# Three buffers instead of two for the split weight panels of a mixture-of-experts stage

## The chip, the cores and the metric

The kernel runs on one NeuronCore of a Trainium2 chip. The metric is the device time of one execution in microseconds (us). TensorE is called PE here, its weight loads PEld, VectorE DVE, ScalarE ACT, GpSimd POOL, and SyncE SP.

## The reference

Two blocks of a network on 256 tokens of width 2048, all in float32. The first is a convolution mixer and a SwiGLU feed-forward. The second is a mixer with gates, and then a hierarchical mixture of experts: a softmax picks one of 4 groups for each token, a second one two of the 4 experts of that group. Only this last part touches the change. Cut down:

```python
pg, g_idx = lax.top_k(p_group, 1)                      # one group of four
pe, e_idx = lax.top_k(softmax(sel_logits), 2)          # two of its four experts
hid = silu(einsum('td,edf->tef', t, w_gate)) * einsum('td,edf->tef', t, w_up)
y = einsum('tef,efd->td', hid * gate[:, :, None], w_down)   # e = 16 experts, f = 512
```

w_gate and w_up are 2048 x 512 for an expert, w_down is 512 x 2048: 12 MB for each of the 16 experts, all of which are read.

## The kernel before

**Precision.** A float32 product is made of three products of a reduced form (fp32r). ACT copies a weight panel into `whi` (the high half), DVE subtracts it from the panel and writes the remainder to `wlo` (the low half). The tokens are split the same way. PE then computes high tokens x high weights, low tokens x high weights, high tokens x low weights.

**Panels.** All weights pass in panels of 128 partitions x 2048 float32, 1 MB each. SP issues one transfer for each into a ring of raw buffers: four (`RING`, the tensor `raw`) in most of the kernel, six (`SLOTS`; `more_raw` holds the other two) in the expert jobs, where the memory of `xT` has come free. A raw buffer may be filled again when DVE has subtracted (`lo_ready`). `whi` and `wlo` have two buffers each, chosen by s % 2.

**Jobs.** The tokens of one group form a job. `GROUPS` is 4, and a group of more than 128 tokens would need one more job; in this trace there are four jobs, called 0 to 3 here. A job has 48 panels (`JOB`): for each of its 4 experts four gate panels, four up panels and four down panels, with the down panels of an expert behind the gate and up panels of the next. A gate or up panel takes 8 products with the high half (line L2635) and 4 with the low half (L2640); a down panel has both at L2652, and the last one of a job at L2666 and L2671. The first panel of the first job is `MOE` in the count of all panels.

**Who waits for whom.** Each engine works through its instructions in the order in which they are written, and counts on semaphores. For panel s of a job that begins at panel n:

- ACT (`expert_hi`, L724; for the first two panels of jobs 1 to 3, L1262) waits for PE's high products (`whi_used`) of the panel that had the buffer before, for DVE's subtraction of it (`lo_ready`), and for the transfer (`raw_in`).
- DVE (`expert_lo`, L1299) waits until PE is through with that earlier panel (`mm_done`) and ACT with this one (`hi_ready`).
- PE waits for `hi_ready`, runs the high products, adds to `whi_used`, waits for `lo_ready`, runs the low products, adds to `mm_done`.

```python
def expert_lo(n, s):
    v.wait_ge(mm_done, n + (s - 1))
    v.wait_ge(hi_ready, n + (s + 1))
    V.tensor_tensor(wlo[:, s % 2, :], expert_raw(s), whi[:, s % 2, :], ALU.subtract).then_inc(lo_ready, 1)
```

Between panels the engines do a job's other work, at fixed places of their order:

- After an expert's gate panels PE turns the hidden rows of the expert before (`turn_hidden`, L2678). ACT copies them (`turned_hi`, L1181) and then takes the sigmoid of the gate's sums (`silu_gate`, L1186), before it splits the seventh panel of the eight. DVE makes their low half (`turned_lo`, L1957) and multiplies (L2013).
- After the up panels DVE multiplies the hidden rows (`hidden`, L2019).
- Over the last eight panels of a job DVE scales four chunks of the next job's token rows (`scaled_row`, L1970). PE turns each chunk (L2627), ACT copies it (L1176), DVE makes its low half (`gathered_lo`, L1952).
- Over the first panels of a job DVE adds the down sums of the job before to its rows, in four chunks (L1995), ACT squares each (L1165), and the root follows (L728). DVE writes the scaled rows in the loop over the experts (L2008). POOL fetches the next job's rows and sends the finished ones.

Some of ACT's functions need another table, which takes an ACT_TABLE_LOAD.

In the first job the tokens' high halves, `tH`, lie in `xT` behind `more_raw`. PE gathers the job's tokens from them (L2615, `gath_done` counts the four parts); after that the memory is not used. The first two low halves of the first job are made by POOL.

Of the kernel before, what the change touches and what calls it, by code (L numbers as in the profile page):

```python
# [20 lines left out]
ALU = mybir.AluOpType  # L21
ACT = mybir.ActivationFunctionType
AX_X = mybir.AxisListType.X
F32 = mybir.dt.float32
F32R = mybir.dt.float32r
# [3 lines left out]
P = 128  # L29
PANEL = 2048  # L30
RING = 4
SLOTS = 6
BANK = 512
# [31 lines left out]
def build_program(  # L65
# [13 lines left out]
    NC = D // BANK  # L79
# [14 lines left out]
    DE = w_exp_gate_2.shape[3]  # L94
# [8 lines left out]
    B = A + 2 * KT  # L103
# [9 lines left out]
    MOE = G + KT  # L113
# [12 lines left out]
    with ctx:  # L126
        arena_at = -(-nc.sbuf_base // 32) * 32

        def sb(name, shape, dt=F32):
            return ctx.enter_context(nc.sbuf_tensor(name, shape, dt))  # L130

        def sem(name):
            return ctx.enter_context(nc.semaphore(name))

        BIG = FT * T
# [6 lines left out]
        whi = sb("whi", [P, 2, PANEL], F32R)  # L142
        wlo = sb("wlo", [P, 2, PANEL], F32R)
# [16 lines left out]
        ps = ctx.enter_context(nc.psum_tensor("ps", [P, 8, BANK], F32))  # L160
# [2 lines left out]
        xTA = xT[:, :].rearrange("p (k c) -> p k c", k=KT)  # L163
        xT5 = xT[:, 0:KT * BANK].rearrange("p (k c) -> p k c", k=KT)
        more_raw = nc.alloc_sbuf_tensor_at("more_raw", [P, SLOTS - RING, PANEL], F32, offset=arena_at + 4 * (BIG + (RING + 2 + 2) * PANEL))
        tH = xT[:, (SLOTS - RING) * PANEL:(SLOTS - RING) * PANEL + TOK * D].rearrange("p (t d) -> p t d", t=TOK)
        uext = big[:, 0:KT * EXT].rearrange("p (k c) -> p k c", k=KT)
        conv_at = KT * EXT + 32
# [17 lines left out]
        xg = moe_r[:, 0:2 * KT * P].rearrange("p (o k c) -> p o k c", o=2, k=KT)  # L186
# [56 lines left out]
        def expert_raw(s):  # L243

            return raw[:, s % SLOTS, :] if s % SLOTS < RING else more_raw[:, s % SLOTS - RING, :]

        def expert_landed(s, r):

            return r * 16 + (16 * (s // SLOTS + 1) + (16 * (MOE // RING) if s % SLOTS < RING else 0))

        raw_in = [sem(f"raw_in{i}") for i in range(SLOTS)]
        hi_ready = sem("hi_ready")
        lo_pool = sem("lo_pool")
        lo_ready = sem("lo_ready")
        mm_done = sem("mm_done")
        whi_used = sem("whi_used")
# [90 lines left out]
        gath_done = sem("gath_done")  # L347
# [359 lines left out]
        def _(a):  # L707
            own = Tally(act_own)
            fn = nc.scalar.activation
# [8 lines left out]

            def expert_hi(n, s, r):

                a.wait_ge(whi_used, n + (s - 1 - MOE))
                a.wait_ge(lo_ready, n + (s - 1 - B))
                a.wait_ge(raw_in[s % SLOTS], expert_landed(s, r))
                fn(whi[:, s % 2, :], expert_raw(s), ACT.Copy).then_inc(hi_ready, 1)  # L724

            def root(src, dst, scale, eps):

# [12 lines left out]
            for src, at in ((norm_mix_pre, V_PRE), (conv_b_in, V_BIN), (conv_b_dw, V_BDW), (conv_ln_g, V_LG),  # L740
                            (conv_ln_b, V_LB), (norm_ffn_pre, V_FPRE), (norm_mix_g_2, V_MIX2)):
                r = src.rearrange("a (k p) -> (a k) p", p=P)
# [336 lines left out]
            for q in range(4):  # L1079
                src = yc if q < 2 else tiles[:, UT:UT + CT, :]  # L1080
                k = (q % 2) * 4
# [80 lines left out]
            def z_square(count, c):  # L1162

                a.wait_ge(z_done, count + c + 1)
                fn(osq[c], orow[:, c * BANK:(c + 1) * BANK], ACT.Square,  # L1165
                   accum_out=st[:, SSQ + c:SSQ + c + 1]).then_inc(z_sq, 1)

            def z_root(count):
                a.wait_ge(z_sum, count)
                root(st[:, SS:SS + 1], st[:, RT:RT + 1], 1.0 / D, st[:, EPS_AT:EPS_AT + 1])  # L1170
# [12 lines left out]
            def silu_gate(done):  # L1183

                a.wait_ge(mm_done, done)
                fn(gsl, ps[:, 0, :], ACT.Sigmoid).then_inc(sig_g, 1)  # L1186
# [69 lines left out]
            def job(jb, more=True):  # L1256
                n = jb * JOB + MOE
                rj = jb * (JOB // SLOTS)
                for s in range(2):
                    a.wait_ge(mm_done, n + (s - 1))  # L1260
                    a.wait_ge(raw_in[s], expert_landed(s, rj))
                    fn(whi[:, s, :], expert_raw(s), ACT.Copy).then_inc(hi_ready, 1)  # L1262
                for c in range(NC):
                    expert_hi(n, 2 + c, rj)
                    z_square(jb * NC, c)
                silu_gate(n + 4)
                expert_hi(n, 6, rj)
                expert_hi(n, 7, rj)
                z_root(jb)
                job_rest(jb, n, more)  # L1270

            with a.Fori(1, last) as jb:
                job(jb)
            job(last, False)
            warm(5)
            for c in range(NC):
# [9 lines left out]
        def _(v):  # L1286
            own = Tally(dve_own)
            V = nc.vector
# [5 lines left out]

            def expert_lo(n, s):

                v.wait_ge(mm_done, n + (s - 1))
                v.wait_ge(hi_ready, n + (s + 1))
                V.tensor_tensor(wlo[:, s % 2, :], expert_raw(s), whi[:, s % 2, :], ALU.subtract).then_inc(lo_ready, 1)  # L1299

            def flat(x3):
                return x3.rearrange("p k c -> p (k c)")
# [430 lines left out]
            for q in range(4):  # L1733
                src = yc if q < 2 else tiles[:, UT:UT + CT, :]
                k = (q % 2) * 4
# [416 lines left out]
        def _(pe):  # L2152
            mm = nc.tensor.matmul
# [33 lines left out]
            for k in range(KT):  # L2187
# [7 lines left out]
                for t in range(TOK):  # L2195
                    i = mm(b[:, META + t * P:META + (t + 1) * P], h[:, t, k * P:(k + 1) * P], x_d[:, t, :], start=True, stop=True)
# [15 lines left out]
            for r in range(1, 6):  # L2212
                rows_in = P if r < 4 else (TAPS * KT - 3 * P if r == 4 else 3 * CT + KT)
                at = ps[:, 7, (r - 1) * P:(r - 1) * P + rows_in] if r < 5 else ps[:, 6, 0:rows_in]
                i = tr(at, vst[0:rows_in, r, :], ident[0:rows_in, 0:rows_in])
# [61 lines left out]
            def column_sum(half, src):  # L2277
                return mm(ps[:, 7, half * T:(half + 1) * T], ones[:, :], src, start=False, stop=True, skip_group_check=True)
# [22 lines left out]
            for m in range(2):  # L2301
                pe.wait_ge(sq_ready, PAIRS + m)
                i = column_sum(1, sq_buf[:, m * T:(m + 1) * T])
# [163 lines left out]
            for s in range(2):  # L2467
# [4 lines left out]
                for k in range(KT):  # L2472
                    i = mm(ps[:, 4 + s, 0:T], wlo[:, s, k * P:(k + 1) * P], xT5[:, k, 0:T], start=False, stop=(k == KT - 1))
# [13 lines left out]
            for q in range(8):  # L2487
# [8 lines left out]
                def banks(o, w):  # L2496
                    for t in range(TOK):
                        for c in range(2):
                            for k in range(2):
                                i = mm(ps[:, 2 * t + c, :], xT5[:, 2 * q + k, o * T + t * P:o * T + (t + 1) * P],  # L2500
                                       w[:, q % 2, k * SW + c * BANK:k * SW + (c + 1) * BANK],
                                       start=False, stop=True, skip_group_check=True)
                    return i
# [22 lines left out]
            for hd in range(HEADS):  # L2526
                for t in range(TOK):
                    at = (hd % 2) * T + t * P
                    i = mm(ps[:, hd // 2, at:at + P], vbuf[:, t, hd * P:(hd + 1) * P], wsT[:, hd, :], start=True, stop=True)
# [53 lines left out]
            for c in range(NC):  # L2583
                i = logits(1, c)
# [45 lines left out]
            def in_panel(n, s, q, bank):  # L2630

                pe.wait_ge(hi_ready, n + (s + 1))
                for o in range(2):
                    for k in range(4):
                        i = mm(ps[:, bank, :], xg[:, o, 4 * q + k, :], whi[:, s % 2, k * DE:(k + 1) * DE],  # L2635
                               start=(q == 0 and o == 0 and k == 0), stop=False)
                i.then_inc(whi_used, 1)
                pe.wait_ge(lo_ready, n + (s + 1 - B))
                for k in range(4):
                    i = mm(ps[:, bank, :], xg[:, 0, 4 * q + k, :], wlo[:, s % 2, k * DE:(k + 1) * DE],  # L2640
                           start=False, stop=(q == 3 and k == 3))
                i.then_inc(mm_done, 1)

# [4 lines left out]
            def down_panel(n, s, r, src):  # L2648

                def banks(o, w):  # L2650
                    for c in range(NC):
                        i = mm(ps[:, 4 + c, :], src[:, o, r, :], w[:, s % 2, c * BANK:(c + 1) * BANK],  # L2652
                               start=False, stop=True, skip_group_check=True)
                    return i
                pe.wait_ge(hi_ready, n + (s + 1))
                banks(0, whi)
                banks(1, whi).then_inc(whi_used, 1)
                pe.wait_ge(lo_ready, n + (s + 1 - B))
                banks(0, wlo).then_inc(mm_done, 1)

            def last_down_panel(n, s, r, src):

                pe.wait_ge(hi_ready, n + (s + 1))
                for o in range(2):
                    for c in range(NC):
                        i = mm(ps[:, 4 + c, :], src[:, o, r, :], whi[:, s % 2, c * BANK:(c + 1) * BANK],  # L2666
                               start=False, stop=True, skip_group_check=True)
                i.then_inc(whi_used, 1)
                pe.wait_ge(lo_ready, n + (s + 1 - B))
                for c in range(NC):  # L2670
                    i = mm(ps[:, 4 + c, :], src[:, 0, r, :], wlo[:, s % 2, c * BANK:(c + 1) * BANK],  # L2671
                           start=False, stop=True, skip_group_check=True)
                    i.then_inc(y_full if c < NC - 1 else mm_done, 1)

# [149 lines left out]
```

## Time and profile before

| | |
|---|---|
| median of 3 runs | 2301.48 us (2299.57 to 2301.8) |
| profiled execution, its own time | 2302.63 us |
| its span in the profile | 2300.9 us |
| busy: PE, PEld, DVE, ACT, POOL | 99%, 84%, 70%, 53%, 11% of the span |
| granted clock of PE, mean | 0.989 of full speed |
| DMA, mean over the span | 514.93 MB, 224 GB/s |
| expert jobs | about 1728 to 2289 us of the span |

The span reaches from the first to the last instruction. A share of busy time is a mean over stages with different limits, so the stage of the expert jobs is read by itself. A matmul's end is modelled; its weight load has both ends recorded.

### The profile page before, as it was taken

How to read it: one execution, taken by the hardware profiler on the slowest of the kernel's cores; microseconds unless marked ns; L12 is line 12 of the kernel's file. 1: busy time of each engine (PE TensorE's matmuls, PEld its weight loads, DVE VectorE, ACT ScalarE, POOL GpSimd, SP SyncE). 2: the span in 40 equal slices, each digit the busy share in tenths (PEclk: the TensorE clock that was granted, in tenths of full speed). 3: DMA queues.
4: the chain of work that ended last, by engine and by line, in shares of the span. 5: the costliest groups of instructions: out<-in, count | busy, mean ns of one | idle time of the engine just before them, and what ended most of it. 6: DMA issues, size and time to landing. Idle time of an engine off the chain costs nothing.

```text
span 2300.9 us, 34667 instructions
## 1 busy us (share of the span) xinstructions
PE 2267.9 (99%) x12099; PEld 1941.2 (84%) x12099; DVE 1610.5 (70%) x1910; ACT 1211.7 (53%) x1229; POOL 248.1 (11%) x107
## 2 busy tenths in 40 slices
PE   9999999999999999999999999999999999999997
PEld 8999688888888888888888888888887877878776
DVE  2999776656556654444586665567458898989987
ACT  4445356444444444344554444444346778687786
POOL 4898101000000000000100000000010000101001
PEclk9999799999999999999999999999989999999999
DMA  7665255666666665555567666655557999999995
GB/s 200 177 180 169 92 198 167 184 192 191 182 191 192 183 192 184 189 198 188 180 197 197 173 183 190 193 165 192 187 207 271 388 357 355 375 364 375 360 366 232
DMA packets 446150, 514.93 MB, mean 224 GB/s; under 512 B 12911, under 2 KB 407847, under 8 KB 410279
## 3 DMA queue, kind: packets, MB, share of 16 engines
q1 hardware_dynamic: 443268, 502.21, 67.1%
q0 software_dynamic: 2544, 11.66, 1.3%
q8 instruction: 39, 0.64, 0.1%
q10 hardware_dynamic: 272, 0.20, 0.0%
q14 instruction: 27, 0.22, 0.0%
HBM read 512.36 MB, written 6.29 MB: 225 GB/s over the span
## 4 chain that ended last, share of the span: by engine, by line
PE 88%; DVE 6%; issue 3%; ACT 3%; POOL 1%; DVEq 0%; ACTq 0%; POOLq 0%
PE ps L2426 25%; PE ps L2320 16%; PE ps L2431 13%; PE ps L2635 9%; PE ps L2652 5%; PE ps L2640 5%; DVE wlo L1299 2%; PE ps L2500 2%; PE ps L2239 2%; PE ps L2221 2%; PE ps L2222 2%; ACT whi L717 1%; DVE ps L1373 1%; PE ps L2333 1%; POOL wlo L547 1%
## 5 line engine op out<-in xcount | busy, mean ns | idle before, releaser
L717 ACT ACTIVATE whi<-raw 128x2048 fp32r<-128x2048 f32 x286 | 547.4, 1914 | 363.2 <-PE ps L2320 189.1
L1293 DVE TENSOR_TENSOR wlo<-raw,whi 128x2048 fp32r<-128x2048 f32 x248 | 567.7, 2289 | 205.3 <-ACT whi L717 205.3
L2426 PE MATMUL ps<-xT,whi 128*128 128x512 f32 x2656 | 638.3, 391 | 5.3 <-DVE xT L1737 4.3
L2426 PEld LDWEIGHTS ps<-xT,whi 128*128 128x128 f32 x2656 | 487.8, 189 | 99.7 <-issue 4.4
L2431 PEld LDWEIGHTS ps<-xT,wlo 128*128 128x128 f32 x2656 | 343.1, 191 | 14.3
L2431 PE MATMUL ps<-xT,wlo 128*128 128x256 f32 x2656 | 347.3, 283 | 0.0
L1299 DVE TENSOR_TENSOR wlo<-raw,whi 128x2048 fp32r<-128x2048 f32 x126 | 287.3, 2289 | 34.8 <-ACT whi L724 30.3
L978 ACT ACTIVATE wk<-ps 128x256 f32<-128x256 f32 x184 | 68.8, 383 | 449.2 <-PE ps L2431 448.9
L724 ACT ACTIVATE whi<-raw 128x2048 fp32r<-128x2048 f32 x120 | 228.5, 1916 | 66.0 <-PE ps L2652 32.9
L2320 PE MATMUL ps<-whi,act 128*128 128x512 f32 x1088 | 260.7, 392 | 0.0
L2635 PE MATMUL ps<-whi,moe_r 128*128 128x512 f32 x1024 | 258.0, 394 | 0.3 <-issue 0.3
L2320 PEld LDWEIGHTS ps<-whi,act 128*128 128x128 f32 x1088 | 206.2, 190 | 44.0 <-issue 0.8
L2635 PEld LDWEIGHTS ps<-whi,moe_r 128*128 128x128 f32 x1024 | 191.2, 189 | 42.1 <-issue 2.5
L1563 DVE TENSOR_TENSOR wk<-ps,wk 128x256 f32<-128x256 f32 x184 | 78.0, 424 | 125.7 <-ACT wk L978 123.7
L1373 DVE SCALAR_TENSOR_TENSOR ps<-big,vT,ps 128x256 f32<-128x256 f32 x410 | 162.1, 481 | 0.0
L1299 DVE TENSOR_TENSOR wlo<-more_raw,whi 128x2048 fp32r<-128x2048 f32 x64 | 146.3, 2291 | 14.6 <-ACT whi L724 14.4
L547 POOL TENSOR_TENSOR wlo<-raw,whi 128x2048 fp32r<-128x2048 f32 x32 | 148.2, 4633 | 30.7 <-ACT whi L717 30.4
L724 ACT ACTIVATE whi<-more_raw 128x2048 fp32r<-128x2048 f32 x64 | 122.8, 1918 | 47.2 <-PE ps L2635 34.4
L2640 PE MATMUL ps<-wlo,moe_r 128*128 128x512 f32 x512 | 139.8, 395 | 3.0 <-DVE wlo L1299 2.4
L1440 DVE TENSOR_TENSOR act<-big,act 128x256 fp32r<-128x256 f32 x60 | 25.3, 425 | 161.4 <-ACT act L896 161.4
L2320 PE MATMUL ps<-wlo,act 128*128 128x512 f32 x544 | 134.4, 389 | 0.0
L2221 PE MATMUL ps<-xT,whi 128*128 128x272 f32 x480 | 121.6, 289 | 0.9 <-DVE vT L1334 0.9
(329 smaller groups left out, 2259.2 us busy)
## 6 DMA issues: line engine op xcount, KB each, us to landing
raw<-in_w_in SPq DMA_DIRECT2D x72, 1024.0 KB, 5.4
raw<-in_w_exp_up SPq DMA_DIRECT2D x56, 1024.0 KB, 6.9
raw<-in_ffn_w_gate SPq DMA_DIRECT2D x44, 1024.0 KB, 5.5
raw<-in_ffn_w_up SPq DMA_DIRECT2D x44, 1024.0 KB, 5.5
raw<-in_ffn_w_down SPq DMA_DIRECT2D x44, 1024.0 KB, 4.8
raw<-in_w_exp_gate SPq DMA_DIRECT2D x40, 1024.0 KB, 6.8
raw<-in_conv_w_in SPq DMA_DIRECT2D x32, 1024.0 KB, 6.0
more_raw<-in_w_exp_down SPq DMA_DIRECT2D x32, 1024.0 KB, 7.5
```

Of the source, the lines that this page charges most:

```text
L547: pool.tensor_tensor(wlo[:, s % 2, :], raw[:, s, :], whi[:, s % 2, :], ALU.subtract).then_inc(lo_pool, 1)
L717: fn(whi[:, s % 2, :], raw[:, s % RING, :], ACT.Copy).then_inc(hi_ready, 1)
L724: fn(whi[:, s % 2, :], expert_raw(s), ACT.Copy).then_inc(hi_ready, 1)
L1293: V.tensor_tensor(wlo[:, s % 2, :], raw[:, s % RING, :], whi[:, s % 2, :], ALU.subtract).then_inc(lo_ready, 1)
L1299: V.tensor_tensor(wlo[:, s % 2, :], expert_raw(s), whi[:, s % 2, :], ALU.subtract).then_inc(lo_ready, 1)
L1373: ins = V.scalar_tensor_tensor(out=accs[m], in0=src, scalar=w, in1=accs[m], op0=ALU.mult, op1=ALU.add)
L2221: mm(ps[:, bank, 0:TM], w, xTA[:, k, 0:TM], start=(k == 0), stop=False)
L2320: i = mm(ps[:, t * NC + c, :], act[:, s % 2, part, t * P:(t + 1) * P], w[:, s % 2, c * BANK:(c + 1) * BANK], start=False, stop=True, skip_ ...
L2426: mm(ps[:, bank, :], whi[:, s % 2, at:at + P], xT5[:, k0 + k, :], start=(k == 0), stop=False)
L2431: i = mm(ps[:, bank, 0:T], wlo[:, s % 2, at:at + P], xT5[:, k0 + k, 0:T], start=False, stop=(k == count - 1))
L2635: i = mm(ps[:, bank, :], xg[:, o, 4 * q + k, :], whi[:, s % 2, k * DE:(k + 1) * DE], start=(q == 0 and o == 0 and k == 0), stop=False)
L2640: i = mm(ps[:, bank, :], xg[:, 0, 4 * q + k, :], wlo[:, s % 2, k * DE:(k + 1) * DE], start=False, stop=(q == 3 and k == 3))
```

## The change

`whi` and `wlo` get a third buffer in the expert jobs. It is a new tensor `third` with two panels, in `xT` right behind `more_raw`, which is where the first job's `tH` lies. Two helpers choose the buffer by s % 3, and 48 is a multiple of 3, so that the choice is the same in each job. The waits on the panel that had the buffer before move from s-2 to s-3, which is one less in each count. Panel 2 of the first job is the first in `third`; its split waits for the end of the gather instead.

```diff
+        third = nc.alloc_sbuf_tensor_at("third", [P, 2, PANEL], F32R, offset=arena_at + 4 * (BIG + (SLOTS + 2 + 2) * PANEL))
...
+        def expert_whi(s):
+
+            return whi[:, s % 3, :] if s % 3 < 2 else third[:, 0, :]
+
+        def expert_wlo(s):
+
+            return wlo[:, s % 3, :] if s % 3 < 2 else third[:, 1, :]
...
             def expert_hi(n, s, r):
 
-                a.wait_ge(whi_used, n + (s - 1 - MOE))
-                a.wait_ge(lo_ready, n + (s - 1 - B))
+                if isinstance(n, int) and n == MOE and s == 2:
+                    a.wait_ge(gath_done, NC)
+                else:
+                    a.wait_ge(whi_used, n + (s - 2 - MOE))
+                    a.wait_ge(lo_ready, n + (s - 2 - B))
                 a.wait_ge(raw_in[s % SLOTS], expert_landed(s, r))
-                fn(whi[:, s % 2, :], expert_raw(s), ACT.Copy).then_inc(hi_ready, 1)
+                fn(expert_whi(s), expert_raw(s), ACT.Copy).then_inc(hi_ready, 1)
...
                 for s in range(2):
-                    a.wait_ge(mm_done, n + (s - 1))
+                    a.wait_ge(mm_done, n + (s - 2))
                     a.wait_ge(raw_in[s], expert_landed(s, rj))
...
             def expert_lo(n, s):
 
-                v.wait_ge(mm_done, n + (s - 1))
+                v.wait_ge(mm_done, n + (s - 2))
                 v.wait_ge(hi_ready, n + (s + 1))
-                V.tensor_tensor(wlo[:, s % 2, :], expert_raw(s), whi[:, s % 2, :], ALU.subtract).then_inc(lo_ready, 1)
+                V.tensor_tensor(expert_wlo(s), expert_raw(s), expert_whi(s), ALU.subtract).then_inc(lo_ready, 1)
```

In `in_panel`, `down_panel` and `last_down_panel` PE reads `expert_whi(s)` and `expert_wlo(s)` in place of the buffers by s % 2; its waits and its order are as before. SP's and POOL's code isn't touched.

## Rows read from the trace of the kernel before

**Rows 1.** The windows view, job 1: busy us of each engine, granted clock, DMA share, GB/s

```profile
1894.80:2035.00 140.20, 139.37 (x621) 111.27 (x621) 127.77 (x85) 108.28 (x78) 6.83 (x2) 1.00 0.97 365
```

**Rows 2.** The waits view of PEld, 1757 to 2289 us: total us, times, longest

```profile
PEld ps L2640 <- DVE wlo L1299: 8.4, 22, 0.7
PEld ps L2652 <- DVE wlo L1299: 7.4, 18, 0.8
```

**Rows 3.** The timeline, an undisturbed panel: start us, us, engine, line

```profile
1792.84 1.92 ACT L724 ACTIVATE whi<-more_raw 128x2048 fp32r<-128x2048 f32 x1 [0.82 <-PE ps L2635]
...
1794.80 2.29 DVE L1299 TENSOR_TENSOR wlo<-more_raw,whi 128x2048 fp32r<-128x2048 f32 x1 [0.45 <-ACT whi L724]
1794.98 0.87 PEld L2640 LDWEIGHTS ps<-wlo,moe_r 128*128 128x128 f32 x4
...
1795.89 1.77 PEld L2635 LDWEIGHTS ps<-whi,moe_r 128*128 128x128 f32 x8
...
1797.70 0.87 PEld L2640 LDWEIGHTS ps<-wlo,moe_r 128*128 128x128 f32 x4
```

**Rows 4.** The timeline, behind a turn of the hidden rows

```profile
1906.61 1.92 ACT L724 ACTIVATE whi<-raw 128x2048 fp32r<-128x2048 f32 x1 [0.78 <-PE ps L2635]
...
1907.19 0.60 PE L2678 MATMUL ps<-ident,tmp 128*128 128x128 f32 x4
...
1908.44 0.58 ACT L1181 ACTIVATE moe_r<-ps 128x512 fp32r<-128x512 f32 x1
...
1909.04 1.28 ACT L1186 ACT_TABLE_LOAD   x1
...
1910.82 3.71 ACT L724 ACTIVATE whi<-raw 128x2048 fp32r<-128x2048 f32 x2
...
1912.77 4.49 DVE L1299 TENSOR_TENSOR wlo<-raw,whi 128x2048 fp32r<-128x2048 f32 x2 [0.71 <-ACT whi L724]
1912.90 1.77 PEld L2635 LDWEIGHTS ps<-whi,moe_r 128*128 128x128 f32 x8
...
1915.11 0.76 PEld L2640 LDWEIGHTS ps<-wlo,moe_r 128*128 128x128 f32 x4 [0.44 <-DVE wlo L1299]
...
1915.92 1.80 PEld L2635 LDWEIGHTS ps<-whi,moe_r 128*128 128x128 f32 x8
```

**Rows 5.** The lines view of DVE, job 1: xcount, busy us, mean ns, idle before

```profile
L1970 DVE SCALAR_TENSOR_TENSOR tmp<-h,st,gB 128x512 f32<-128x512 f32 x4 | 4.5, 1136 | 0.0
...
L1952 DVE TENSOR_TENSOR moe_r<-ps,moe_r 128x512 fp32r<-128x512 f32 x4 | 2.7, 683 | 0.0
```

**Rows 6.** The timeline, the start of job 2 and the longest wait

```profile
2012.02 1.77 PEld L2635 LDWEIGHTS ps<-whi,moe_r 128*128 128x128 f32 x8
...
2016.60 0.68 DVE L1995 TENSOR_TENSOR moe_o<-ps,h 128x512 f32<-128x512 f32 x1
...
2019.40 0.68 DVE L1995 TENSOR_TENSOR moe_o<-ps,h 128x512 f32<-128x512 f32 x1
...
2132.90 0.76 PEld L2652 LDWEIGHTS ps<-wlo,moe_r 128*128 128x128 f32 x4 [0.83 <-DVE wlo L1299]
```

**Rows 7.** The timeline, the first job's panels 2 and 4

```profile
1735.99 2.28 DVE L1299 TENSOR_TENSOR wlo<-raw,whi 128x2048 fp32r<-128x2048 f32 x1
...
1738.33 0.76 PEld L2640 LDWEIGHTS ps<-wlo,moe_r 128*128 128x128 f32 x4 [2.19 <-DVE wlo L1299]
...
1746.02 0.76 PEld L2640 LDWEIGHTS ps<-wlo,moe_r 128*128 128x128 f32 x4 [0.77 <-DVE wlo L1299]
```

**Rows 8.** The windows view, timeline and landing: the transfers

```profile
1970.00:1985.00 15.00, 15.00 (x70) 12.40 (x69) 13.48 (x8) 11.46 (x8) 0.00 (x0) 1.00 1.02 418
...
2108.79 0.33 SPq L494 DMA_DIRECT2D raw<-in_w_exp_up  x1
...
DMA to landing us min/median/max: 12.0/12.0/12.0
...
2121.32 1.92 ACT L724 ACTIVATE whi<-raw 128x2048 fp32r<-128x2048 f32 x1 [0.80 <-PE ps L2635]
```

More of the change, by code:

```diff
@@ L2634, in in_panel @@
                     for k in range(4):
-                        i = mm(ps[:, bank, :], xg[:, o, 4 * q + k, :], whi[:, s % 2, k * DE:(k + 1) * DE],
+                        i = mm(ps[:, bank, :], xg[:, o, 4 * q + k, :], expert_whi(s)[:, k * DE:(k + 1) * DE],
                                start=(q == 0 and o == 0 and k == 0), stop=False)
@@ L2639, in in_panel @@
                 for k in range(4):
-                    i = mm(ps[:, bank, :], xg[:, 0, 4 * q + k, :], wlo[:, s % 2, k * DE:(k + 1) * DE],
+                    i = mm(ps[:, bank, :], xg[:, 0, 4 * q + k, :], expert_wlo(s)[:, k * DE:(k + 1) * DE],
                            start=False, stop=(q == 3 and k == 3))
@@ L2651, in banks @@
                     for c in range(NC):
-                        i = mm(ps[:, 4 + c, :], src[:, o, r, :], w[:, s % 2, c * BANK:(c + 1) * BANK],
+                        i = mm(ps[:, 4 + c, :], src[:, o, r, :], w[:, c * BANK:(c + 1) * BANK],
                                start=False, stop=True, skip_group_check=True)
@@ L2655, in down_panel @@
                 pe.wait_ge(hi_ready, n + (s + 1))
-                banks(0, whi)
-                banks(1, whi).then_inc(whi_used, 1)
+                banks(0, expert_whi(s))
+                banks(1, expert_whi(s)).then_inc(whi_used, 1)
                 pe.wait_ge(lo_ready, n + (s + 1 - B))
-                banks(0, wlo).then_inc(mm_done, 1)
+                banks(0, expert_wlo(s)).then_inc(mm_done, 1)
             def last_down_panel(n, s, r, src):
@@ L2665, in last_down_panel @@
                     for c in range(NC):
-                        i = mm(ps[:, 4 + c, :], src[:, o, r, :], whi[:, s % 2, c * BANK:(c + 1) * BANK],
+                        i = mm(ps[:, 4 + c, :], src[:, o, r, :], expert_whi(s)[:, c * BANK:(c + 1) * BANK],
                                start=False, stop=True, skip_group_check=True)
@@ L2670, in last_down_panel @@
                 for c in range(NC):
-                    i = mm(ps[:, 4 + c, :], src[:, 0, r, :], wlo[:, s % 2, c * BANK:(c + 1) * BANK],
+                    i = mm(ps[:, 4 + c, :], src[:, 0, r, :], expert_wlo(s)[:, c * BANK:(c + 1) * BANK],
                            start=False, stop=True, skip_group_check=True)
```

## The prediction

> **What bounds the kernel now.** I first read the page's forty slices. From about 1750 us on they are another kernel: the rows of DMA and GB/s jump, DVE's and ACT's rise, PE's stays full. That stretch is the expert jobs, the only code that the diff touches. The trace holds four jobs of 48 panels, 192 in all. The windows view then says which engine sets the pace: in job 1 (the second) PE is busy 139.37 of 140.20 us at a granted clock of 1.00, DVE 127.77, ACT 108.28, and the core moves 365 GB/s [rows 1]. PE is the bound; a "busy" PE can still lose time, because the end of a matmul is modelled. So the timeline of PE's weight loads (PEld) is the one to read: each matmul has one load, and a gap between loads is lost time.
>
> Where nothing is late, the eight products with the high half take 1.81 us, the four with the low half 0.91 us, and a panel 2.72 us [rows 3]. The waits view of PEld over 1757 to 2289 us holds 22 waits of 8.4 us in the gate/up panels and 18 of 7.4 us in the down panels for DVE's subtraction that makes the low half [rows 2]. No wait for a high half and none for a DMA is in it. So 40 waits, 15.8 us, stand between PE and its full pace.
>
> They cost less than they last. In row group 4 the high products start at 1912.90, so the low ones were due at 1914.71; they start at 1915.11 (0.40 late), and the next panel would start at 1915.92 where 1915.62 was due: the four loads after a wait go 0.10 faster. A wait noted as 0.44 costs 0.30 us; the note is 0.14 too long. Forty waits cost 15.8 - 40 x 0.14 = 10.2 us. This is what is at stake here.
>
> **Why the low half is late.** For panel 22 of job 0, ACT starts the high half at 1792.84, 0.82 us after idling for PE, ends it at 1794.76; DVE takes 1794.80 to 1797.09; PE wants the low half at 1797.70 [rows 3]. The margin is 0.61 us. With two buffers ACT may not start panel s until PE's high products of s-2 have been read, so neither ACT nor DVE can build up more than this 0.61 us, though a panel needs only 1.92 us of ACT and 2.29 of DVE out of 2.72. Any other DVE work above 0.61 us plus the slack is passed on to PE: 1.14 us for a gain-scaled chunk of token rows, 0.68 for the low half of gathered columns [rows 5].
>
> **The change part by part.** Nothing is computed anew, no instruction is added but the choice of a buffer, which is made when the program is built. The panel arithmetic, the DMA count (192 of 1 MB) and their order stay. So no cost is added in work; all of it is a shift of waits.
>
> 1. *Waits of ACT and DVE one panel back* (whi_used, lo_ready and mm_done at s-2 in place of s-1). ACT and DVE may run up to 2.72 us further ahead. The margin goes from 0.61 to at most 3.33 us. The longest of the forty waits in the timeline is 0.83 us, in panel 41 of job 2 [rows 6]; the burst behind it has used up 0.61 + 0.83 = 1.4 us of margin: under 3.33. Over a job DVE has 140.2 - 127.8 = 12.4 us idle [rows 1]; after a gain of 3.4 a job there are still 9 left, so the lead can be rebuilt: (2.72 - 2.29) = 0.43 us a panel.
>
> 2. *The in-order stretches*, where more buffers don't help by themselves, since ACT's and DVE's queues hold an instruction that needs PE. I walk the three kinds.
>  After PE turns the hidden rows (once an expert), ACT's order is: split of the panel before, copy of the turned rows, a table load, the sigmoid, split of the next panel. In row group 4 the split at 1906.61 runs to 1908.53 and pushes the copy to 1908.44, though the turn's last matmul ended at 1907.79; the load follows at 1909.04, and the splits at 1910.82, DVE at 1912.77, ending 1915.06 for a due time of 1914.71. With a third buffer the split of 1906.61 is done a panel earlier, the copy starts at about 1907.9, and the rest moves with it by 0.5 us: the low half ends at about 1914.5. The 0.35 us that it was too late is covered, by 0.15 us only.
>  At the end of a job DVE carries four chunks of scaled rows (4 x 1.14), four low halves of gathered columns (4 x 0.68), a hidden-row product (0.7) and the low half of the turned rows (0.7) beside eight panels: 8 x 2.29 + 8.7 = 27.0 us, against 8 x 2.72 + about 2.5 of PE's turns = 24.3. It runs 2.7 us behind over this stretch; the lead of up to 3.33 takes it up with little left. The same order of instructions laid out by hand, with each one's wait on PE or ACT, gives every low half in time, the tightest (panel 45) by about 0.0 us.
>  At the start of a job DVE takes a chunk of the finished rows (0.68) between panels, and chunk to chunk is 2.80 us (2016.60 to 2019.40) [rows 6] for PE's 2.72: DVE loses 0.08 a panel for four panels. The first chunk stands 4.6 us behind PE's first load of the job (2012.02) now [rows 6], and by the same laying out about 3 us behind it after. Panel 9, which comes after the root of the final norm and two table loads on ACT, is again in time by about 0.0 us.
>  I therefore take 0.3 us a job for what the two tight places still cost: 3 x 0.3 = 0.9 us. Its bounds are 0 (the walk is right) and 4.2 us (rival 1).
>
> 3. *Panel 2 of the first job waits for the gather's end* instead of for whi_used and lo_ready. Its split is not held up by either: the low half of panel 2 starts at 1735.99, behind DVE's low half of the last gathered columns, and PE waits 2.19 us for it until 1738.33 [rows 7]. That order is not edited. This wait, and one of 0.77 us two panels on [rows 7], which lies behind a chain of small routing instructions in DVE's order, stay. Gain at the start: 0; bounds 0 and the 2.7 us that both cost. PE's own order has the whole gather ahead of panel 0, which is two panels earlier, so the new wait costs nothing.
>
> 4. *The transfers.* A panel's raw buffer is freed by DVE, so the transfers start earlier by as much as DVE runs ahead, and are wanted earlier by as much. The total supply must rise from 48 panels in 140.2 us (2.92 us each) to 48 in 136.8 (2.85). A stretch with the queue full moved 418 GB/s over 15 us: 1.0486 MB in 2.51 us [rows 8]. So there is room. The tightest place is after the fetch of the next job's rows: a panel issued at 2108.79 landed 12.0 us later, at 2120.79, and ACT took it at 2121.32 [rows 8], 0.53 us later. ACT will meet the transfer there and wait, but it spends its lead, not PE's time. Cost 0; bound above by rival 3.
>  The Trainium skill (DMA: Bandwidth & Descriptors, Where 436 GB/s comes from) says that for transfers from HBM to SBUF the HBM side binds at about 358 GB/s. By that rule the jobs, at 365 GB/s, would already be at their limit and the sum of this change 0. The row of 418 GB/s over 15 us disagrees; the section above it on the same page gives 358 as the share with both cores of a pair streaming.
>
> **The sum.** 10.2 - 0.9 + 0 = 9.3 us. The profiled execution took 2302.63 us (span 2300.9 and 1.7 around it), so 2293.3 for such a one; its time is 1.15 over the median of the three runs, 2301.48, so the median comes to 2292.2 us, 0.40% less.
>
> **The rivals.**
> 1. *ACT's serial stretches keep their stalls.* Four places a job (two turns of hidden rows with a table load, the loop's start with another, the root of the final norm) are set by ACT's order, not by buffers. For it: before the split at 1910.82 ACT did not idle [rows 4]. Against: the copy ahead of it was delayed by a split that the third buffer moves. At 0.30 each, with 3.5 jobs' worth: 4.2 us stay, the gain is 6.0, the time 2295.5.
> 2. *The change does nothing that counts*: DMA share is 0.97 in job 1 [rows 1], supply is at its limit, and the waits for DVE turn into waits for transfers. Time 2301. The Trainium skill's 358 GB/s (same section) would make this the case. Against: 418 GB/s [rows 8], and even at the tightest place a landed panel lies 0.53 us before ACT takes it, while ACT's idle time is named by PE.
> 3. *Slower*: with ACT, DVE and transfers bunched at the job's ends, the transfers come less evenly than now, and PE waits for high halves. The place is panels 38 to 41 of jobs 1 and 2 after the fetch, with 0.53 us in hand. It decides when the mean landing interval exceeds today's 2.92 us a panel; at 2.95 it costs 0.03 x 188 = 5.6 us: 2307. Against: 2.51 us a panel was reached in just such a stretch, behind the fetch of job 1.
> 4. *More*: the start's two waits vanish too, and no tight place costs: 10.2 + 2.7 = 12.9, 2288.6. Against: DVE's order there is not touched.
>
> **How the numbers follow.** Forecast 0.66, rival 1 0.17, rival 2 0.10, rival 3 0.05, rival 4 0.02. The likeliest gives 2292.2. Its own range is 2290.5 to 2294.5. The range for eight in ten reaches from rival 4's 2288.5 to 2299, halfway from rival 1 to no change. A measurement of this kernel tells about 0.2% (4.6 us) from no change, so "faster" is below 2296.9: the forecast, rival 4 and, with 6.0 us of gain, most of rival 1: 0.81. "Same" gets rival 2 and the weak end of rival 1: 0.14. Slower: 0.05.
>
> **What the changed profile would show.** The waits view of PEld over the jobs should fall from 15.8 us in 40 waits to under 3 us, with those left behind panels 9 and 45 or after a hidden turn. A job should last about 137 us. The start should still show its waits of some 2.2 and 0.8 us. ACT's idle time should be named more by transfers or by older panels. Splits should begin up to 2.7 us further ahead of PE; ACT's 1.92 and DVE's 2.29 us should not change. I would be wrong if PE shows waits for high halves or ACT waits of microseconds for landings that reach PE, if the splits become longer, or if the waits after hidden turns stay at 0.4.

## The result and the profile after

The change makes the kernel faster: 2287.16 us, the median of 5 runs (2285.26 to 2288.57), against 2301.65 (2299.57 to 2301.96). The comparison of the runs gives a ratio of 0.9942, with a 95% interval of 0.9931 to 0.9953 (the two medians alone give 0.9937). The forecast was 2292.2 with a range of 2288.5 to 2299: right in sign and mechanism, too small by 5 us, and the median lies below the range. The profiled execution took 2285.31 us.

The page of the changed kernel: the span, and busy time, share and instructions of the engines.

```profile
span 2283.6 us, 34678 instructions
...
PE 2254.0 (99%) x12099; PEld 1943.3 (85%) x12099; DVE 1607.3 (70%) x1910; ACT 1208.3 (53%) x1229; POOL 248.0 (11%) x107
```

The work of DVE and ACT is what it was (1610.5 and 1211.7 us before), so nothing was saved in work. PE's line has 13.9 us less in it (2267.9 before) for the same 12099 matmuls: it counts time in which a matmul runs slowly or waits, so the sum of busy time alone doesn't say where it went.

The windows view of jobs 0, 1 and 2 (cut at the first product of each job's bank clearing): length, busy us of PE, PEld, DVE, ACT and POOL, granted clock, DMA share, GB/s.

```profile
1750.80:1886.90 136.10, 135.90 (x617) 112.00 (x617) 124.77 (x86) 102.13 (x74) 2.24 (x1) 1.00 0.96 373
1886.90:2023.50 136.60, 136.60 (x622) 112.38 (x622) 126.73 (x86) 107.18 (x78) 6.83 (x2) 1.00 0.97 374
2023.50:2160.10 136.60, 136.60 (x622) 112.41 (x622) 127.20 (x86) 107.76 (x78) 6.83 (x2) 1.00 0.97 378
```

Job 1 lasts 136.6 us against 140.2 [rows 1], and PE is busy in all of it. PEld's busy time rose from 111.27 to 112.38 for the same loads, and that is no loss: the four loads behind a wait take 0.76 us together in place of 0.87 [rows 3, rows 4], and there are fewer of them. DMA moves 374 GB/s against 365.

The waits view of PEld over the jobs of the changed kernel: total us, times, longest.

```profile
PEld ps L2647 <- issue: 1.5, 3, 0.6
PEld ps L2238 <- issue: 1.1, 3, 0.4
PEld ps L2647 <- ACT whi L736: 0.8, 2, 0.4
```

The forty waits for DVE of [rows 2] are gone, every one. What is left stands where it stood before: the clearing of the banks, the loops' ends. The two waits put down to ACT's split are no late high halves. Each is the 0.42 us behind the clearing of the banks, which is in the kernel before as well and is called "issue" there.

The timeline behind a turn of the hidden rows, the place of [rows 4] in the same job.

```profile
1898.66 0.58 PEld L2690 LDWEIGHTS ps<-ident,tmp 128*128 128x128 f32 x4
1898.89 0.60 PE L2690 MATMUL ps<-ident,tmp 128*128 128x128 f32 x4
...
1899.52 0.60 ACT L1193 ACTIVATE moe_r<-ps 128x512 fp32r<-128x512 f32 x1 [2.01 <-PE ps L2690]
1900.14 1.28 ACT L1198 ACT_TABLE_LOAD   x1
...
1901.43 0.60 ACT L1198 ACTIVATE tmp<-ps 128x512 f32<-128x512 f32 x1
...
1901.92 1.91 ACT L736 ACTIVATE third<-raw 128x2048 fp32r<-128x2048 f32 x1
...
1903.87 2.29 DVE L1311 TENSOR_TENSOR third<-raw,third 128x2048 fp32r<-128x2048 f32 x1 [1.12 <-ACT third L736]
...
1904.59 1.77 PEld L2647 LDWEIGHTS ps<-third,moe_r 128*128 128x128 f32 x8
...
1906.08 2.28 DVE L1311 TENSOR_TENSOR wlo<-raw,whi 128x2048 fp32r<-128x2048 f32 x1
...
1906.40 0.87 PEld L2652 LDWEIGHTS ps<-third,moe_r 128*128 128x128 f32 x4
...
1908.28 2.29 DVE L1311 TENSOR_TENSOR wlo<-more_raw,whi 128x2048 fp32r<-128x2048 f32 x1
```

ACT now idles ahead of the copy (L1193) and starts it at 1899.52, where PE's turn ends at 1899.49. In [rows 4] it began 0.65 us after the end of the turn, held up by a split. The rest of ACT's order is as before. DVE's low half of panel 14 runs from 1903.87 to 1906.16, and PE wants it at 1906.40: 0.24 us to spare, where it was 0.35 late. The subtractions behind it start 2.20 us apart (1906.08, 1908.28), though each is listed with 2.28 or 2.29 us. So DVE gains 0.52 us on a panel of 2.72 us when it doesn't wait.

The transfers at their tightest place, after the fetch of the next job's rows in job 2. In [rows 8] ACT's idle time was still named by PE; now ACT's timeline has:

```profile
2107.98 1.92 ACT L736 ACTIVATE whi<-more_raw 128x2048 fp32r<-128x2048 f32 x1 [0.44 <-DMA more_raw<-in_w_exp_down]
2110.52 1.92 ACT L736 ACTIVATE third<-more_raw 128x2048 fp32r<-128x2048 f32 x1 [0.62 <-DMA more_raw<-in_w_exp_down]
2113.01 1.92 ACT L736 ACTIVATE whi<-raw 128x2048 fp32r<-128x2048 f32 x1 [0.57 <-DMA raw<-in_w_exp_down]
```

In panels 40 to 42 ACT waits for transfers, 0.4 to 0.6 us each, and PE sees nothing of it.

The start of the first job, where the forecast said nothing would change (DVE's low half of panel 2, then PEld):

```profile
1729.83 2.28 DVE L1311 TENSOR_TENSOR third<-raw,third 128x2048 fp32r<-128x2048 f32 x1
...
1732.16 0.77 PEld L2652 LDWEIGHTS ps<-third,moe_r 128*128 128x128 f32 x4 [2.19 <-DVE third L1311]
...
1735.22 0.77 PEld L2652 LDWEIGHTS ps<-wlo,moe_r 128*128 128x128 f32 x4 [0.47 <-DVE wlo L1311]
...
1739.84 0.76 PEld L2652 LDWEIGHTS ps<-wlo,moe_r 128*128 128x128 f32 x4 [2.02 <-DVE wlo L1311]
```

The 2.19 us are the same as in [rows 7]. The 0.77 became 0.47 and 2.02: in this execution the granted clock was 1.00 where the one before had a short stretch at a lower level (a mean of 0.66 over 1738 to 1743 us), and PE met DVE's routing chain sooner. The change has no part in it: the unchanged kernel shows 0.46 and 1.99 us in one of its later executions, at a clock of 1.00. From the first product of panel 0 to the clearing of the banks both kernels take 27.8 us, so the start gave nothing.

**Where the time went.** The two profiled spans differ by 17.3 us, more than the medians. At the first product of panel 0 the changed kernel is already 6.2 us ahead (1722.0 against 1728.2), and it is 5.0 of that ahead at the first product of the convolution's output projection (257.1 against 262.1), in code that the change doesn't touch. From panel 0 to the last panel it takes 549.6 us against 560.7: 11.1 us. So two questions are open: what are the 6 us, and which part of the change gave the 11.

### The profile page after: what moved, and what is told of

The parts are those of the page before. It is cut to its first block, busy times and chain, and to the rows that moved or that the text cites. A ratio compares the mean times of both kernels' runs of the same rounds, so it can differ in the third digit from the quotient of the medians.

```text
span 2283.6 us, 34678 instructions
## 1 busy us (share of the span) xinstructions
PE 2254.0 (99%) x12099; PEld 1943.3 (85%) x12099; DVE 1607.3 (70%) x1910; ACT 1208.3 (53%) x1229; POOL 248.0 (11%) x107
## 4 chain that ended last, share of the span: by engine, by line
PE 92%; DVE 3%; issue 2%; ACT 2%; POOL 1%; DVEq 0%; ACTq 0%; POOLq 0%
PE ps L2438 25%; PE ps L2332 16%; PE ps L2443 13%; PE ps L2647 10%; PE ps L2664 7%; PE ps L2652 5%; PE ps L2512 2%; PE ps L2251 2%; PE ps L2233 2%; PE ps L2234 2%; ACT whi L726 1%; DVE ps L1385 1%; PE ps L2345 1%; POOL wlo L556 1%; PE ps L2174 1%
## 5 line engine op out<-in xcount | busy, mean ns | idle before, releaser
L726 ACT ACTIVATE whi<-raw 128x2048 fp32r<-128x2048 f32 x286 | 547.4, 1914 | 359.6 <-PE ps L2332 184.8
L1305 DVE TENSOR_TENSOR wlo<-raw,whi 128x2048 fp32r<-128x2048 f32 x248 | 567.8, 2289 | 205.4 <-ACT whi L726 205.4
L1311 DVE TENSOR_TENSOR wlo<-raw,whi 128x2048 fp32r<-128x2048 f32 x94 | 214.2, 2288 | 3.9 <-ACT whi L736 3.5
L736 ACT ACTIVATE whi<-raw 128x2048 fp32r<-128x2048 f32 x88 | 168.1, 1914 | 32.2 <-PE ps L2647 23.1
L2647 PE MATMUL ps<-whi,moe_r 128*128 128x512 f32 x672 | 168.2, 392 | 0.2 <-issue 0.2
L556 POOL TENSOR_TENSOR wlo<-raw,whi 128x2048 fp32r<-128x2048 f32 x32 | 147.8, 4623 | 31.2 <-ACT whi L726 30.9
L2647 PEld LDWEIGHTS ps<-whi,moe_r 128*128 128x128 f32 x672 | 124.8, 188 | 26.0 <-issue 0.6
L2233 PE MATMUL ps<-xT,whi 128*128 128x272 f32 x480 | 121.8, 289 | 0.9 <-DVE vT L1346 0.9
L2234 PE MATMUL ps<-xT,whi 128*128 128x272 f32 x480 | 121.5, 287 | 0.0
L2332 PEld LDWEIGHTS ps<-wlo,act 128*128 128x128 f32 x544 | 102.1, 188 | 21.2
L649 POOL TENSOR_TENSOR wlo<-raw,whi 128x2048 fp32r<-128x2048 f32 x4 | 18.3, 4589 | 833.7 <-DVE h L1498 833.4
```

Source lines behind the costliest of these rows:

```text
L556: pool.tensor_tensor(wlo[:, s % 2, :], raw[:, s, :], whi[:, s % 2, :], ALU.subtract).then_inc(lo_pool, 1)
L726: fn(whi[:, s % 2, :], raw[:, s % RING, :], ACT.Copy).then_inc(hi_ready, 1)
L736: fn(expert_whi(s), expert_raw(s), ACT.Copy).then_inc(hi_ready, 1)
L1305: V.tensor_tensor(wlo[:, s % 2, :], raw[:, s % RING, :], whi[:, s % 2, :], ALU.subtract).then_inc(lo_ready, 1)
L1311: V.tensor_tensor(expert_wlo(s), expert_raw(s), expert_whi(s), ALU.subtract).then_inc(lo_ready, 1)
L2233: mm(ps[:, bank, 0:TM], w, xTA[:, k, 0:TM], start=(k == 0), stop=False)
```

## The experiments

The stage "jobs" below is the time from the first product of panel 0 to the start of the last product of the last panel, read from each run's own profile. "Ahead" is the start of panel 0.

**Controls.** No edit; the two kernels again, first in several runs and later in one profiled execution more.

> The kernel before, unchanged, as a control. The profile of the changed kernel stands 17.3 us ahead of the one before when the last panel is through: 6.2 us of it at 335 us of the span, long ahead of the expert jobs, and 11.1 within them. Theory A: the 6.2 us are chance: the stretch in which PE is granted half the clock around 245 to 280 us was 23.9 us long in one execution and 10.2 in the other, and its length differs between executions of one kernel; in some executions of this control it is short too, and the first panel of the expert jobs starts near 1722 instead of 1728. Theory B: the stretch is long in every execution of this kernel and short in those of the changed one, since the program's size or place changed; then this control shows 1728 again and a ratio of 1.000. The time by both: 2300 to 2302, by A with some runs down to 2296.

> The changed kernel again, unchanged. Expert jobs, from the first load of panel 0 to the end of the last panel: 549.7 us as in its first profile, within 0.5. The part ahead of them: by theory A between 1722 and 1728 us, by theory B 1722. Time 2285 to 2289 by B, up to 2291 by A.

Measured: the kernel before 2302.23 us (2298.96 to 2304.03, 12 runs), ahead 1728.2, jobs 560.9; the same kernel, run beside it as the reference of the comparison, 2301.35 with 23 runs from 2296.3 to 2304.15; ratio 1.0002 (0.9993 to 1.0010). The changed kernel 2290.56 us (2285.48 to 2293.1, 6 runs), ratio 0.9946 (0.9932 to 0.9959), ahead 1726.9, jobs 549.9. The jobs repeat to 0.2 us. The part ahead differed by 4.9 us between two executions of the changed kernel.

> The kernel before, one look more at the length of the half-clock stretch: 10 to 24 us by theory A, with jobs of 560.8 us in either case; always 20 or more by theory B.

> The changed kernel, one look more: jobs of 549.8 us; the stretch of half clock ahead 10 to 24 us long.

Measured: the kernel before ahead 1723.7, jobs 560.8; the changed one ahead 1727.7, jobs 549.7. So this time the unchanged kernel had the short part ahead and the changed one the long. The windows view at the end of the convolution (the last three columns are granted clock, DMA share, GB/s) for the kernel before:

```profile
245.00:255.00 10.00, 10.00 (x20) 4.62 (x19) 4.42 (x7) 1.37 (x3) 0.00 (x0) 0.66 0.29 105
255.00:265.00 10.00, 10.00 (x30) 6.04 (x29) 8.26 (x15) 2.86 (x7) 0.56 (x1) 0.66 0.39 128
265.00:275.00 10.00, 10.00 (x46) 8.28 (x45) 6.94 (x13) 5.19 (x6) 0.00 (x0) 1.00 0.29 100
```

and for the changed kernel, on the same chip:

```profile
245.00:255.00 10.00, 10.00 (x16) 4.67 (x15) 3.65 (x7) 1.22 (x2) 0.00 (x0) 0.50 0.28 105
255.00:265.00 10.00, 10.00 (x21) 4.60 (x20) 8.26 (x15) 2.75 (x7) 0.56 (x1) 0.50 0.43 135
265.00:275.00 10.00, 10.00 (x40) 8.03 (x40) 3.61 (x10) 2.73 (x4) 0.00 (x0) 0.87 0.18 76
```

The first runs 20 us at a mean of 0.66 and is then at full speed; the second is at 0.50, the lower of TensorE's two levels, 1.2 GHz, for the whole 20 us and beyond (0.87 over the next ten). The unchanged kernel had 0.50 there too in its two executions before this one. What PE does there is the same in both, column sums and products with one row. Theory A holds: the length of this stretch varies from execution to execution, in both kernels.

**The high half alone, the low half alone.**

```diff
 # hi_only, on the changed kernel
-            return wlo[:, s % 3, :] if s % 3 < 2 else third[:, 1, :]
+            return wlo[:, s % 2, :]
...
-                v.wait_ge(mm_done, n + (s - 2))
+                v.wait_ge(mm_done, n + (s - 1))
```

> Three high halves, two low halves as before: ACT may run a panel further ahead, DVE waits as before for PE to be through with panel s-2. By my forecast's reasoning the low half is late from DVE's bursts (end and start of a job) and from ACT's order (after the turn of the hidden rows, after the root). With ACT alone ahead, the second kind goes and the first stays. Of the 11.0 us that the jobs gained, I expect 3 to 6. Rival: both halves of the change are needed together, since DVE's own wait on PE keeps it from using an early high half: then under 2 us. Second rival: the high half alone gives nearly all, over 9.

Measured: 2288.28 us (2285.85 to 2293.41), ratio 0.9944 (0.9931 to 0.9957), ahead 1723.7, jobs 550.2. PEld's only waits for DVE in the jobs behind the start, and DVE's waits for PE:

```profile
PEld ps L2664 <- DVE wlo L1311: 0.5, 2, 0.3
```

```profile
DVE wlo L1311 <- PE ps L2652: 18.2, 46, 0.4
...
DVE wlo L1311 <- PE ps L2664: 3.8, 10, 0.4
```

My figure of 3 to 6 us was wrong; the second rival holds, the high half alone gives 10.7 of the 11.1. DVE does wait for PE now, 56 times and 22 us in all, and it costs 0.4. I had the margins of the two buffers confused. With two high halves ACT may start a split when PE has used the one two panels back, and ACT's 1.92 and DVE's 2.29 us both lie behind that. With two low halves only DVE's 2.29 us lie behind the wait: the timeline of this kernel has it at one panel as

```profile
1785.98 2.29 DVE L1311 TENSOR_TENSOR wlo<-raw,whi 128x2048 fp32r<-128x2048 f32 x1 [0.43 <-PE ps L2664]
1787.29 0.87 PEld L2652 LDWEIGHTS ps<-wlo,moe_r 128*128 128x128 f32 x4
```

and PE wants this low half at 1790.01, behind the next panel's. That is 1790.01 - 1788.27 = 1.7 us of margin, where the longest wait of before had asked for 1.4.

```diff
 # lo_only, on the changed kernel: two high halves with the waits of before
-            return whi[:, s % 3, :] if s % 3 < 2 else third[:, 0, :]
+            return whi[:, s % 2, :]
...
-                    a.wait_ge(whi_used, n + (s - 2 - MOE))
-                    a.wait_ge(lo_ready, n + (s - 2 - B))
+                a.wait_ge(whi_used, n + (s - 1 - MOE))
+                a.wait_ge(lo_ready, n + (s - 1 - B))
...
-                    a.wait_ge(mm_done, n + (s - 2))
+                    a.wait_ge(mm_done, n + (s - 1))
```

> Three low halves, two high halves as before: DVE may run ahead, but ACT still waits for PE's high products of s-2 and gives DVE a high half only 2.9 us before PE wants the low one. I expect at most 1 us of the 11.0, since the waits view says that DVE idled for ACT's split and not for PE. Rival: DVE's bursts gain from it as well, 3 to 6 us.

Measured: 2297.84 us (2296.15 to 2303.74, 12 runs), ratio 0.9993 (0.9982 to 1.0004), ahead 1724.9, jobs 560.8. The waits of PEld over the jobs behind the start, and DVE's:

```profile
PEld ps L2661 <- DVE wlo L1308: 5.2, 15, 0.7
PEld ps L2649 <- DVE third L1308: 5.0, 13, 0.5
PEld ps L2649 <- DVE wlo L1308: 3.2, 8, 0.7
...
PEld ps L2661 <- DVE third L1308: 2.3, 3, 0.8
```

```profile
DVE third L1308 <- ACT whi L733: 25.0, 33, 2.2
DVE wlo L1308 <- ACT whi L733: 19.9, 48, 0.9
```

39 waits of 15.7 us, as in [rows 2]; DVE waits for ACT's split as before. The third low half gives nothing by itself.

**How much lead there is.** DVE makes one low half twice, that of the first down panel (16 and 28) of two experts in each job, 8 times in all.

```diff
+                if twice is not None:
+                    V.tensor_tensor(wlo[:, s % 2, :], expert_raw(s), whi[:, s % 2, :], ALU.subtract).then_inc(lo_once, 1)
+                    v.wait_ge(lo_once, twice)
```

> The kernel before, with one subtraction of DVE (2.29 us, and about 0.1 for a wait on itself) done twice, in the first down panel of each expert in the loop: 8 places in the four jobs, one panel ahead of the hidden rows' product and, in jobs 1 to 3, of two scaled chunks. With two high halves DVE's margin is 0.61 us, and in jobs 1 to 3 it is used up there. Expected: the jobs grow by 13 to 19 us over 560.7. It measures the margin, not a computed result: the output is the same.

> Three high and two low halves, with the same double subtraction. High halves give 0.61 + 2.72 = 3.3 us of margin; the wait of DVE for PE to be through with panel s-2 leaves 0.91 or less: lo(s) may start when panel s-2 is through, and PE wants it 2.72 + 1.81 = 4.5 us later, so 2.2 us of margin beside the subtraction. If that is the bound, a burst of 2.4 us alone costs 0.2, and 2.4 + 2.2 us in jobs 1 to 3 about 1.5 at each of 6 places: jobs 550.1 + 5 to 11. If two low halves were no bound at all: + 0 to 3.

> Three high and three low halves, with the same double subtraction. Margin 3.3 us from the high halves and 4.9 from the low ones. If the third low half is worth something when DVE's bursts are longer, the jobs grow less than with two: 549.8 + 0 to 6, and below the run with three high halves alone. Rival: the same as that one, then the third low half is worth nothing here either.

Measured, in one execution each: 2313.88, 2298.72 and 2301.64 us; jobs 572.8, 560.0 and 558.6 us, so + 12.0, + 9.8 and + 8.8 over the same kernels without the edit. The line with most of PEld's waits in each, in that order:

```profile
PEld ps L2656 <- DVE wlo L1303: 20.7, 26, 1.8
```

```profile
PEld ps L2668 <- DVE wlo L1315: 13.0, 23, 1.2
```

```profile
PEld ps L2668 <- DVE wlo L1315: 10.9, 18, 1.2
```

The first is below what I expected, the second inside, the third above. With three buffers of each a burst of 2.4 us should have vanished in a margin of 3.3. In job 0 it did: its two places have no wait, and the job got 0.1 us longer. The 18 waits stand at the six places of jobs 1 to 3, and each of these jobs got 2.9 us longer, 1.5 us a place. So the 3.3 us are not there in panel 16 of those jobs. The timeline of the third kernel shows it, in job 1:

```profile
1917.53 1.77 PEld L2668 LDWEIGHTS ps<-whi,moe_r 128*128 128x128 f32 x8
...
1918.11 2.29 DVE L1315 TENSOR_TENSOR wlo<-more_raw,whi 128x2048 fp32r<-128x2048 f32 x1
1920.32 2.29 DVE L1315 TENSOR_TENSOR third<-more_raw,third 128x2048 fp32r<-128x2048 f32 x1
...
1920.45 0.76 PEld L2668 LDWEIGHTS ps<-wlo,moe_r 128*128 128x128 f32 x4 [1.15 <-DVE wlo L1315]
```

PE's high products begin at 1917.53, so the low ones were due at 1919.34. The low half of panel 16 is there only at 1920.4. Without the second subtraction it would have been there at 1918.1, so the lead was 1.2 us, not 3.3. Two panels before, behind the turn of the hidden rows, the lead is 0.24 us (above), and it is 0.2 with two low halves as well: ACT has to wait there for PE's turn and then has a copy, a table load and a sigmoid ahead of its next split. From there it grows by the 0.52 us that DVE gains on a panel. In job 0 the same turn has no table load behind it (ACT copies at 1762.44, takes the sigmoid at 1762.93 and splits at 1763.41). The changed kernel without the double subtraction shows there, again for panel 14:

```profile
1765.36 2.29 DVE L1311 TENSOR_TENSOR third<-raw,third 128x2048 fp32r<-128x2048 f32 x1 [0.18 <-ACT third L736]
...
1769.30 0.87 PEld L2652 LDWEIGHTS ps<-third,moe_r 128*128 128x128 f32 x4
```

The low half is there at 1767.65, a lead of 1.65 us, and by panels 19 to 23 it has grown to 3.3 or 3.4 us, where the buffers end it. The third low half is worth 1.4 us of jobs in this case, 1.0 of them in job 0, where the lead can pass 1.7 us before the burst. It is worth 0.4 without the double subtraction.

**A better start.** DVE's order at the first job's start, on the kernel with three high halves alone.

```diff
-            gathered_lo(0, 3, FIRST_TURN[3])
             expert_lo(MOE, 2)
-            chosen_logits()
+            gathered_lo(0, 3, FIRST_TURN[3])
             expert_lo(MOE, 3)
-            chosen_experts()
+            chosen_logits()
             expert_lo(MOE, 4)
+            chosen_experts()
```

> Three high and two low halves, and DVE's order at the first job's start: the low half of panel 2 ahead of the low half of the last gathered columns, the low halves of panels 3 and 4 each ahead of the routing chain that preceded it. The 2.19 us that PE waits in panel 2 should go (the high half is there 2 us earlier, and DVE idles), and of the 0.47 and 2.02 us behind it some 1 to 1.5 us. Jobs 547 to 548.5 against 550.1. Rival: DVE is the bound over the whole stretch up to panel 8, and the gain at panel 2 is lost again before the gates: 549.5 to 550.

Measured: 2287.57 us (2285.15 to 2292.47), ratio 0.9948 (0.9933 to 0.9962), jobs 549.1. PEld's waits at the start:

```profile
1732.89 0.76 PEld L2652 LDWEIGHTS ps<-wlo,moe_r 128*128 128x128 f32 x4 [0.28 <-DVE wlo L1311]
...
1736.08 0.76 PEld L2652 LDWEIGHTS ps<-wlo,moe_r 128*128 128x128 f32 x4 [0.56 <-DVE wlo L1311]
...
1739.15 0.76 PEld L2652 LDWEIGHTS ps<-wlo,moe_r 128*128 128x128 f32 x4 [0.45 <-DVE wlo L1311]
...
1743.77 0.76 PEld L2652 LDWEIGHTS ps<-wlo,moe_r 128*128 128x128 f32 x4 [2.02 <-DVE wlo L1311]
1745.44 0.52 PEld L2697 LDWEIGHTS ps<-wk,moe_r 128*128 128x128 f32 x4 [0.91 <-DVE wk L1959]
```

The 2.19 us of panel 2 shrank to 0.28, and the same time came back behind it: the rival holds for the most part. The jobs missed the 547 to 548.5 us that I expected. DVE's routing chain has to end before the gates, wherever it stands. The gain is 1.0 us by the stages, and too small for the times to tell: this kernel, the one with three high halves and the changed one are alike.

**The stretch of half clock, filled.** Three matmuls on all rows of the array ahead of each bias product but those of bank 7, on both kernels. The trace has 42 of them, so 14 sets and not the 12 of the expectation.

```diff
+                if bank != 7:
+                    for _ in range(3):
+                        mm(ps[:, bank, 0:P], ones[:, :], ones[:, :], start=True, stop=True)
```

> The kernel before with three more matmuls of 128x128 on all rows of the array ahead of each of 12 one-row bias products between the convolution and its output projection, where PE is granted half the clock for 10 to 24 us. Their results are overwritten. By theory A (the length of that stretch differs between executions, whatever the kernel) full-array work there removes or fixes the stretch: the spread of times, 8 us so far (2296.0 to 2304.2), shrinks to some 2 us, and the first panel of the expert jobs starts at the same time in this kernel and in the changed one with the same edit. The edit itself costs up to 9 us of PE and gives back up to 10. If the stretch stays, nothing is learned from the level.

> The changed kernel with the same edit. Theory A: the part ahead of the expert jobs as in the kernel above, within 1 us, and the time 11.0 us below it (10.5 to 11.5), which is the change by itself. Theory B (the change also shortens the part ahead by some 3 to 6 us): 14 us or more below it.

Measured: 2303.48 us (2300.24 to 2312.07, 12 runs) and 2294.98 (2289.03 to 2302.47, 12 runs), both slower than without the edit. The spread did not shrink, it grew to 12 and 13 us, so the pair did not isolate the change by its times (8.5 us between the medians, 11.2 between the lowest). Theory A had expected the same part ahead in both, within 1 us; it was 1725.8 and 1734.1. Over 245 to 265 us the mean clock was 0.83 in the first and 0.69 in the second, so the stretch was altered and not removed. The jobs took 560.8 and 549.7 us, 11.1 apart, as without the edit.

## Why the prediction was wrong

**What holds.** The bound (PE), the place (the low half is late behind ACT's split), the sign, DMA and the tightest place of the transfers, where ACT waits and PE doesn't, the unchanged 2.19 us at the start, the 0.2 us that a turn of the hidden rows with a table load leaves to spare, and a job of about 137 us were as forecast. By the stages the change is worth 11.1 us.

**The sum was 9.3.** The stage gave 11.1. The 0.9 us for the two tight places, panels 9 and 45, measured 0: no wait stands there. Panel 45's low half is ready within 0.1 us of when it is wanted in jobs 0 to 2, as laid out; panel 9's is 0.6 to 1.1 us early in jobs 1 to 3, where I had 0.0. The forty panels that had a noted wait became 10.5 us shorter, against the forecast 10.2: each wait cost 0.13 us less than its note, short ones and long ones alike, against the 0.14 taken from one of them. Another 0.6 us came from the other panels, which the sum had at nothing: 0.14 in the last panel of job 0, the rest under 0.05 us a panel, too short for the waits view to list. Together 1.8 us; 2290.4 would have been inside the range.

**The step that failed** is in "The sum": the forecast was set on 2301.48, the median of three runs, as if the rest of the kernel stood still. It doesn't. The part ahead of the jobs ended between 1722.0 and 1729.4 us in the profiled executions without the fill, and 6.6 of these 7.4 us arose between the first bias product (near 241 us) and 341 us, around the stretch at half clock. The unchanged kernel took 2296.0 to 2304.15 us over all its 75 runs, the changed one 2285.3 to 2293.1 over its 12: both ends are 11 us apart, as the jobs are. The first three runs of before fell between 2299.6 and 2301.8, the first five of after in their lower half. My range had no term for this, and it was worth 3.4 us: the medians differ by 14.5, the stage by 11.1. That it is chance and not the change's work is shown by the pair of executions in which the unchanged kernel had the shorter part ahead (1723.7 against 1727.7). The later runs agree: the medians of the second comparison are 10.8 us apart.

**Part 1** credited both halves of the change with the lead. It is the third high half; the third low half alone gives 0, and 0.4 us on top of the other.

**The margin of 3.3 us** is what the buffers allow, and panels 19 to 23 of job 0 reach it. It is no figure for the whole job: behind a turn of the hidden rows with a table load, two in each of jobs 1 to 3, it is 0.24. The forecast for those places was right because it was worked out there, and the double subtraction showed what the general figure is worth elsewhere. The rate at which the lead comes back was put too low, at 0.43 us a panel from the listed 2.29 us; subtractions in a row start 2.20 us apart, which gives 0.52.

**The rivals.** The first (ACT's serial stretches keep 4.2 us) fell: those waits are gone, if by 0.24 us. The second and third (supply of transfers) fell: 378 GB/s in job 2. The Trainium skill's 358 GB/s (DMA: Bandwidth & Descriptors, Where 436 GB/s comes from) would have left no gain; the trace disagrees, with 378 GB/s averaged over a whole job. The fourth was right that no tight place would cost; the start's two waits, which it had vanish, stayed.

## What to carry to other kernels

Where one value passes two engines on its way to a third, the buffer to add is the one whose release lies at the head of the chain: its wait covers both engines' work, and the second buffer's covers only the last. A deeper buffer gives lead only up to the next instruction in the same queue that needs the consumer, so the lead has to be worked out at those places, with what follows in that queue (here 0.24 us with a table load behind it, 1.65 without).

Before a forecast of half a per cent, look at where two executions of the same kernel differ, and compare by the stage that was changed: here stages repeated to 0.2 us and whole times to 8.

## What the runs showed of the hardware

The time at half clock around PE's one-row products differed between executions of one program, from a mean clock of 0.66 over 20 us to 0.50 over 20 us and more in the unchanged kernel, with the same instructions ahead of it. Between the starts of their jobs lay 4.5 us (1723.7 against 1728.2), 4.4 of which were there at 341 us. Why it differs stays open. Fourteen sets of three matmuls on the full array in that stretch did not remove it (mean clocks of 0.83 and 0.69), and both kernels became slower, by 3.6 and 4.4 us in their medians.

A noted wait of a weight load is longer than what it costs: the next four loads follow each other 0.10 us faster in all, and forty waits noted with 15.8 us in the unchanged kernel cost 10.5.

DVE's subtractions of 128x2048 are listed with 2.29 us each and start 2.20 us apart when they follow each other without a wait (1906.08, 1908.28).
